# Sums of squares of the late query and key projections: one fp32 matmul replaced by two fp32r matmuls of a rounded part and its remainder

## The reference

```
def rms_norm_2(x, g):
    xf = x.astype(jnp.float32)
    y = xf * lax.rsqrt(jnp.mean(xf * xf, axis=-1, keepdims=True) + EPS) * g.astype(jnp.float32)
    return y.astype(x.dtype)

# even layer                                              # odd layer
q = rms_norm_2(dq.reshape(B, T, 16, 64), q_gain)          q = rms_norm_2(q.reshape(B, T, 32, 64), q_gain)
k = rms_norm_2(dk, k_gain)                                k = rms_norm_2(k.reshape(B, T, 4, 64), k_gain)
```

## Time and profile before

| what | value |
|---|---|
| median of 3 runs | 3009.62 us (3006.83 to 3009.97) |
| the profiled execution's own time | 3007.83 us |
| span of its instructions | 3006.0 us |
| TensorE (PE) busy | 2836.8 us, 94% of the span |
| DVE, ACT, POOL busy | 36%, 31%, 37% |
| mean granted TensorE clock | 0.969 of full |

### The profile page before, as it was taken

One profiled execution on the slowest core, in us unless ns is written; L12 is line 12 of the kernel. 1 busy time (PEld: TensorE's weight loads), 2 busy tenths in 40 slices (PEclk: granted clock), 3 DMA queues, 4 the chain that ended last, 5 costly groups with the idle time before them and its releaser, 6 DMA issues.

```text
span 3006.0 us, 34273 instructions
## 1 busy us (share of the span) xinstructions
PE 2836.8 (94%) x13922; PEld 2176.9 (72%) x13922; DVE 1091.3 (36%) x1796; ACT 927.0 (31%) x1425; POOL 1103.3 (37%) x536
## 2 busy tenths in 40 slices
PE   3679999999998997699999999999999999999999
PEld 1167688878877785357887677766788877777787
DVE  2262133113224402322221447854322465666411
ACT  2031241224124211042222322255422222666411
POOL 3043302341341330024554333444455443445443
PEclk8589999999999998799999999999999999999999
DMA  8914722231238320032434233322344333332442
GB/s 293 351 56 145 228 62 61 68 94 41 71 88 130 84 71 28 14 127 74 123 112 99 70 98 85 91 78 85 123 123 119 84 99 91 85 83 76 137 122 81
DMA packets 459337, 311.94 MB, mean 104 GB/s; under 512 B 32016, under 2 KB 412816, under 8 KB 458416
## 3 DMA queue, kind: packets, MB, share of 16 engines
q1 hardware_dynamic: 425264, 265.41, 30.8%
q10 hardware_dynamic: 33920, 44.37, 5.7%
HBM read 289.71 MB, written 32.10 MB: 107 GB/s over the span
## 4 chain that ended last, share of the span: by engine, by line
PE 89%; DMA 4%; DVE 3%; POOL 2%; ACT 1%; issue 1%; SPq 0%; ACTq 0%; DVEq 0%; POOLq 0%
PE acc L1654 75%; PE aux L1654 7%; PE ssq L1657 3%; PE ssq L1654 3%; DMA ada_ring<-in_w_ada 2%; DMA raw<-in_w_in 1%; POOL normed L1042 1%; DVE x_t L1191 1%; DVE rstd L1222 1%; PE aux L1657 1%; POOL w_lo L1053 1%; DMA masks_sb<-in_masks 1%; ACT staged L727 0%; ACT w_hi L748 0%; DVE p L1283 0%
## 5 line engine op out<-in xcount | busy, mean ns | idle before, releaser
L1053 POOL TENSOR_TENSOR w_lo<-raw,w_hi 128x1024 fp32r<-128x1024 f32 x362 | 869.7, 2403 | 1699.7 <-ACT w_hi L748 1699.7
L1654 PE MATMUL acc<-h_hi,w_hi 128*128 128x512 f32 (+1 forms) x3232 | 1211.0, 392 | 23.4 <-DVE x_t L1191 8.0
L1654 PE MATMUL acc<-h_hi,w_lo 128*128 128x512 f32 (+1 forms) x3232 | 1173.2, 380 | 0.0
L1654 PE MATMUL acc<-h_lo,w_hi 128*128 128x512 f32 (+1 forms) x2464 | 873.0, 376 | 0.8 <-issue 0.8
L748 ACT ACTIVATE w_hi<-raw 128x1024 fp32r<-128x1024 f32 x362 | 383.0, 1059 | 1166.2 <-PE acc L1654 1086.2
L1654 PEld LDWEIGHTS acc<-h_hi,w_hi 128*128 128x128 f32 x3232 | 585.7, 188 | 176.4 <-issue 52.3
L1654 PEld LDWEIGHTS acc<-h_hi,w_lo 128*128 128x128 f32 x3232 | 584.2, 188 | 118.1
L1654 PEld LDWEIGHTS acc<-h_lo,w_hi 128*128 128x128 f32 x2464 | 441.1, 189 | 94.7 <-issue 13.0
L1654 PE MATMUL acc<-out_t_lo,w_hi 128*128 128x512 f32 x768 | 298.9, 389 | 0.0
L1222 DVE RECIPROCAL rstd<-rstd 128x512 f32<-128x512 f32 (+1 forms) x29 | 118.0, 4070 | 407.0 <-ACT rstd L788 407.0
L1654 PEld LDWEIGHTS acc<-out_t_lo,w_hi 128*128 128x128 f32 x768 | 144.3, 188 | 29.1
(11 more groups left out here) (217 smaller groups left out, 2341.1 us busy)
## 6 DMA issues: line engine op xcount, KB each, us to landing
raw<-in_w_in SPq DMA_DIRECT2D x52, 1024.0 KB, 5.8
raw<-in_even_w_in SPq DMA_DIRECT2D x41, 1024.0 KB, 5.5
raw<-in_odd_w_in SPq DMA_DIRECT2D x36, 1024.0 KB, 5.6
ada_ring<-in_w_ada SPq DMA_DIRECT2D x32, 1024.0 KB, 8.7
gate_ring<-in_w_ada SPq DMA_DIRECT2D x16, 1024.0 KB, 7.1
raw<-in_w_out SPq DMA_DIRECT2D x16, 1024.0 KB, 5.9
raw<-in_even_w_out SPq DMA_DIRECT2D x16, 1024.0 KB, 5.8
raw<-in_odd_w_out SPq DMA_DIRECT2D x16, 1024.0 KB, 6.6
```

The costliest lines, as they stand in the source:

```text
L1053: G_.tensor_tensor(WL[half][:], RAW[G.rs][:, half * HALF * P:(half + 1) * HALF * P], WH[half][:].bitcast(F32), ALU.subtract).then_inc(S["l ...
L1654: return M.matmul(out_, lhsT, rhs, start=start, stop=stop, skip_group_check=True)
```

## The change

The 27 sums of squares are made by two fp32r matmuls of one pass each instead of one fp32 matmul. ACT's Square now writes the square rounded to fp32r (`squares_hi`). DVE multiplies `scaled` by itself into `squares` in full fp32 (first new instruction), waits for ACT's rounded square, and subtracts it (second new instruction), which gives the remainder (`squares_lo`) and increments a new semaphore `sq_low`. Both stand directly behind `take` on DVE, ahead of the selection rounds. TensorE waits for `sq_low` where it waited for `sq_made`, and `first` stands behind k-tile 4 instead of 3 when the previous group is of kind `norm` or `kvn`. The ones are copied once into an fp32r tile (`ones64_r`) by DVE in the group `ikw`. Some small tiles move to other addresses.

```
     SQ2, RS2 = at("squares2", SEQ, 174 * K1), at("rstd2", SEQ, 176 * K1)
+    SQH2, SQL2 = at("squares2_hi", SEQ, 194 * K1, F32R), at("squares2_lo", SEQ, 196 * K1, F32R)
+    ONESR = at("ones64_r", P, 200 * K1 + 512, F32R)
...
+        def squares(G):
+            return (SQH3, SQL3) if G.dst in ("K3", "Q3") else (SQH2, SQL2)
...
     elif G.kind in ("norm", "kvn"):                      # ACT, post
         act.wait_ge(S["taken"], G.t + 1)
         need(act, "sq_summed", G.norm)
-        A.activation(scratch(G)[0][:], Y[G.y][:], ACT.Square).then_inc(S["sq_made"], 1)
+        A.activation(squares(G)[0][:], Y[G.y][:], ACT.Square).then_inc(S["sq_made"], 1)
...
     e.then_inc(S["taken"], 1)                            # DVE, take
+    if k in ("norm", "kvn"):
+        SQ, (high, low) = scratch(G)[0], squares(G)
+        dve.wait_ge(S["taken"], G.t + 1)
+        L.link(Vv.tensor_tensor(SQ[:], Y[G.y][:], Y[G.y][:], ALU.mult))
+        dve.wait_ge(S["sq_made"], G.norm + 1)
+        need(dve, "sq_summed", G.norm)
+        Vv.tensor_tensor(low[:], SQ[:], high[:].bitcast(F32), ALU.subtract).then_inc(S["sq_low"], 1)
...
     L.done(Vv.tensor_copy(IDR[:], IDENT[:]))             # DVE, after, ikw
+    L.done(Vv.tensor_copy(ONESR[:], ONES64[:]))
...
     if k in ("norm", "kvn"):                             # TensorE, first
-        pe.wait_ge(S["sq_made"], G.norm + 1)
+        pe.wait_ge(S["sq_low"], G.norm + 1)
         need(pe, "std_made", G.norm)
-        mm(SSQ[:, 0:SEQ], ONES64[:], scratch(G)[0][:], True, True).then_inc(S["sq_summed"], 1)
+        high, low = squares(G)
+        mm(SSQ[:, 0:SEQ], ONESR[:], high[:], True, False)
+        mm(SSQ[:, 0:SEQ], ONESR[:], low[:], False, True).then_inc(S["sq_summed"], 1)
...
-    at_first = 5 if prev is not None and prev.kind == "wout" else 3
+    at_first = 3 if prev is None else {"wout": 5, "norm": 4, "kvn": 4}.get(prev.kind, 3)
```

More of the change, by code:

```diff
@@ L429, in build @@
     Y = [at(f"scaled{s}", SEQ, (201 + 2 * s) * K1) for s in range(2)]
-    LNG, LSM, LRI = (at(n, 16, 200 * K1 + 512 + 64 * i) for i, n in enumerate(("u_neg_max", "u_sum", "u_inv")))
+    LNG, LSM, LRI = (at(n, 16, 200 * K1 + 256 + 64 * i) for i, n in enumerate(("u_neg_max", "u_sum", "u_inv")))
     FIN = [at(f"final{s}", SEQ, 2 * s * K1) for s in range(2)]
@@ L445, in build @@
     PW = at("pool_w_sb", 8 * 256, 144 * K1)
-    TRI = at("tri_sb", P, 200 * K1)
+    TRI = at("tri_sb", P, 198 * K1)
     IDX, WK = at("index_score", QT * SEQ, 80 * K1), at("index_work", 3 * SEQ, 88 * K1)
@@ L455, in build @@
     SQ3, RS3 = at("squares3", SEQ, 180 * K1), at("rstd3", SEQ, 182 * K1)
+    SQH3, SQL3 = at("squares3_hi", SEQ, 184 * K1, F32R), at("squares3_lo", SEQ, 186 * K1, F32R)
     P3 = [at(f"p3_{s}", 4 * 257, 180 * K1 + 4128 * s) for s in range(3)]
     PT3 = at("p3_t", 2 * SEQ, 192 * K1 + 256)
-    T3 = [at(f"win_bias{s}", 256, 196 * K1 + 512 + s * K1) for s in range(4)]
+    T3 = [at(f"win_bias{s}", 256, 196 * K1 + 256 + s * K1) for s in range(4)]
     DST = dict(Q=Q, K=K, V=V, GATE=GATE, KD=KD, Q2=Q2, Q3=Q3)
@@ L488, in build @@
             "bias_ready", "o_hi", "o_lo", "od_hi", "od_lo",
-            "taken", "xg_hi", "xg_lo", "sq_ready", "sum_done", "rstd_ready", "gated", "sq_made", "sq_summed", "std_made",
+            "taken", "xg_hi", "xg_lo", "sq_ready", "sum_done", "rstd_ready", "gated", "sq_made", "sq_low", "sq_summed", "std_made",
             "rs_made", "normed", "y_turned", "y_copied", "pooled", "pool_mm", "py_done", "ot_hi", "ot_lo", "sel_done",
```

## The result

| | before | changed |
|---|---|---|
| median | 3008.44 us (4 runs, 3006.83 to 3009.97) | 3033.57 us (4 runs, 3030.0 to 3036.22) |
| ratio to before | | 1.0082, 95% interval 1.0067 to 1.0096 |
| span of the profiled execution | 3006.0 us | 3034.4 us |

The changed kernel is slower by 0.8%, 25 us. Forecast were 3030.7 us and a range of 3021 to 3043, with a chance of 0.90 for slower.

The account below looks back on a forecast made before the run. TensorE, 89% of the chain, was taken as the bound. 14.7 - 0.4 + 2.7 + 2.2 + 1.7 + 0.2 = +21.1 us on 3007.83 gave 3028.9, with 1.8 for the median 3030.7; range 3021 to 3043.

Parts of the forecast that it names:

- The mechanism: Sum of each group: POOL's remainder of the weights holds DVE's subtraction to about B+4.4 (B: group's first matmul); TensorE waits 1.0 us.
- The saving: TensorE's sum of squares: two single-pass matmuls cost 0.45 us instead of 0.89, saving 0.44 per group, 11.9 for 27.
- The ordinary group: Q2 tiles 1 to 5, first K3, all 16 Q3, met by an idle DVE: +0.67 us each, 22 together +14.7.
- the second key tile of the odd layer: Second K3, DVE late: product falls into POOL's operation, subtraction out at B+5.1 (B: next group's first matmul), +1.36 us.
- Q2 tile 0: First even query tile, its take without idle time before it: product and subtraction both come behind POOL's operation, +1.36 us.
- tile 6: Q2 tile behind the end of the selection: three comparisons and a held product make DVE later, +1.36 to +2.8, taken +2.2.
- the start of the attention: Q2 tile 7, attention unit 1 already waiting 2.01 us: +1.3 for the chain's delay, +0.4 for the clock, together +1.7 us.
- The clock rival: Behind each of 26 TensorE waits the lower clock costs 1.0 us: +26 on top, 3057 us; chance 0.08.
- The faster rival: DVE's subtraction is not held by POOL, out at B+2.6, TensorE waits nowhere: -11.9 us, 2998 with the copy; chance 0.06.
- DVE as the bound: Even tiles: DVE needs 12.9 us per group, more than 12.5; five tiles pay +1.36, +4 to +8, 3035 to 3039; chance 0.10.
- `kvn`: Sum of the `kvn` group: pooling matmuls before the next k-tile 0 hide the subtraction, -0.4 us (at worst +0.7).
- The copy of the ones: In group `ikw`, TensorE waits for DVE's copy of the ones: +0.2 us (0 to 0.6).

## Why the prediction was right, point by point

**The mechanism.** TensorE waits for a subtraction that POOL holds up, ordinary groups lose more than the pair saves, and it repeats without growing. Shown by the changed kernel's own rows, and by turning ACT's order round: 2.48 us became 0.69 and in the ordinary groups the wait went. That the DVE work or its load is the cost there was excluded (odd groups 11.79 us with it), and so was a pair that saves nothing (11.33 us). Only behind the selection is DVE's load itself a cost: with the same work and no wait for the remainder that tile lost 6.0 us.

**The saving.** Forecast 0.44 us for each sum, measured 0.46 (11.79 to 11.33).

**The ordinary group.** Forecast: pair at B+4.4, +0.67. Measured: B+4.46, +0.75, 22 times. POOL hardly noticed the new product: its row is 2.46 us instead of 2.38, not 2.6; it ended at B+3.86, inside the forecast window. The wait was 1.06 us instead of 1.0, and the slower start behind it cost 0.15 instead of 0.1: the pair took 0.57 us up to the next matmul instead of 0.45, and the 33 behind it 7.51 instead of 7.48. 22 x 0.08 = 1.8 us more than forecast.

**The tiles where DVE is late.** For the second key tile of the odd layer I forecast B+5.1 and +1.36; the pair starts 5.1 behind the boundary and the group costs 1.4; TensorE's bracket there is 1.57.

In the even tiles the two late terms were mis-sized. Q2 tile 0 was to cost +1.36 and cost 3.4; tile 6 was to cost +2.2 and cost 4.3. DVE's take and product of tile 0, and its last `q_t` and the take of tile 6:

```profile
1884.83 0.69 DVE L1534 TENSOR_TENSOR scaled<-acc,rstd_n 128x512 f32<-128x512 f32 x1
1885.55 2.04 DVE L1539 TENSOR_TENSOR squares<-scaled 128x512 f32<-128x512 f32 x1
```

```profile
1963.59 1.55 DVE L1603 SCALAR_TENSOR_TENSOR q_t<-scaled,cols_sb,rstd 128x512 f32<-128x512 f32 x1
1965.06 0.68 DVE L1534 TENSOR_TENSOR scaled<-acc,rstd_n 128x512 f32<-128x512 f32 x1
```

In tile 0 it is the product that comes second to POOL and takes 2.04 us; in tile 6 the take stands right behind the `q_t` that the selection had held up.

The waits that follow, on TensorE, ahead of the pair of tile 0 and of tile 1, and ahead of that of tile 6 and of attention unit 1:

```profile
1888.37 0.50 PE L1669 MATMUL ssq<-squares_hi,ones_r 128*128 128x512 f32 x1 [1.90 <-DVE squares_lo L1542]
...
1902.54 0.50 PE L1669 MATMUL ssq<-squares_hi,ones_r 128*128 128x512 f32 x1 [0.90 <-DVE squares_lo L1542]
```

```profile
1967.24 0.50 PE L1669 MATMUL ssq<-squares_hi,ones_r 128*128 128x512 f32 x1 [2.88 <-DVE squares_lo L1542]
...
1987.50 0.47 PE L1669 MATMUL acc<-select_mask,ident_r 128*128 128x256 f32 x2 [3.35 <-DVE q_t L1603]
```

And what the chain shows behind them (33 matmuls of a group, 7.53 us where the clock is full), with the windows of the clock:

```profile
1889.10 9.15 PE acc L1669 x33
...
1903.28 7.53 PE acc L1669 x33
...
1968.14 8.93 PE acc L1669 x33
```

```profile
1888.50:1891.50 3.00, 3.00 (x9) 2.38 (x10) 2.93 (x10) 0.69 (x1) 0.00 (x0) 0.61 1.10 300
1967.50:1970.50 3.00, 3.00 (x9) 2.29 (x9) 1.61 (x1) 0.69 (x1) 0.00 (x0) 0.52 1.14 326
2362.00:2365.00 3.00, 3.00 (x13) 2.49 (x14) 1.57 (x1) 0.86 (x2) 0.00 (x0) 1.00 1.11 308
2392.00:2582.00 190.00, 176.41 (x760) 141.16 (x760) 140.66 (x77) 50.86 (x61) 72.90 (x30) 1.00 0.32 86
```

Tile 0's wait of 1.90 us was followed by 33 matmuls in 9.15 us, tile 6's wait of 2.88 by 33 in 8.93: 1.6 and 1.4 us that went with the clock, at 0.61 and 0.52 of full in the first 3 us. I had given the clock to one place, the start of the attention, and counted it nowhere else short of the rival. That is the step that was off: I took the waits of the late tiles as ordinary ones, though they were about as long as, or longer than, the one wait of which the earlier trace rows had shown the price. The remaining 0.4 and 0.7 us are mostly the takes, which came later than I took them. Yet no rule by the length of the wait would have given these prices: behind 2.06 us the clock stayed at 1.00 in the kernel with ACT's order turned round and the sum behind k-tile 3, and behind 2.86 us the kernel with DVE's work alone lost 3.0 us, not 1.4. What decides whether and for how long the clock falls stays open; 3.0 of the measured microseconds hang on it.

**The clock rival.** It gave every wait a loss. In the odd tiles the clock is 1.00 over all 190 us with a wait in each group, and it is 1.00 behind the 1.57 us of the second key tile. The Trainium skill (TensorE: Matmul & The Clock Gate, "A second HAM failure mode: psum-queue depth-cycling") tells of a kernel in which frequent short idle times between groups of matmuls made the clock oscillate; 0.91 us in each 12.5 and, with the sum behind k-tile 3, 1.57 in each 13.2 did not do so here.

**The faster rival and DVE as the bound.** The first fell with the row of 2.48 us. The second: in the even tiles 1 to 5 DVE still had about 1 us idle at each boundary, and groups were 12.54 us, as forecast: the last product came behind POOL's operation in 0.75 us. At the boundaries of tile 0 and of the tile behind the selection DVE was late, as forecast.

**The rest.** `kvn` -0.4, forecast -0.4. The start of the attention +1.5, forecast +1.7; its wait was 3.35 us. The copy of the ones 0.1, forecast 0.2.

The sum by what was measured: 22 x 0.754 + 3.4 + 4.3 + 1.4 + 1.5 - 0.4 + 0.1 = 26.9, against 21.1 forecast and 25 between the medians. The two profiled executions differ by 28.4; the 1.5 left over lie ahead of the changed stretch, and cannot be put down to the change: the changed kernel and those of the experiments built from it, which have the same instructions up to there, reach the end of the `kvn` tile at times that lie up to 8.6 us apart. So that the median came within 3 us of the forecast is partly luck: in the stretch that was worked out the forecast was 5.8 us short.

## What to carry to other kernels

Replacing one matmul by two faster ones moves the question from TensorE to whoever makes the second operand: work out when that operand is ready, from the rows of every engine around the boundary, before counting the saving. An elementwise operation of DVE with two inputs in SBUF that is issued while POOL runs one costs POOL's rest plus its own tail; turning round two instructions on a third engine (here ACT's) can take it out of the way for nothing. Where a wait has a fixed end, each matmul moved ahead of it is saved in full. A wait near 2 us may cost the clock too: ask for its price, but don't count on one.

## What the runs showed of the hardware that was not expected

- A single wait of under 2 us can already be followed by the lower clock, and its length alone doesn't say whether it is. Waits with a bracket of 0.91 us (22 in the changed kernel) and 1.57 us (in nearly every group with the sum behind k-tile 3) left the clock at 1.00. Waits of 1.84, 1.90, 2.88 and 4.74 us were followed by 3 us at 0.50 to 0.61 of full. Of waits near 2 us some were followed by the lower clock (2.01 before), others not: 2.06 us with ACT's order turned round and the sum behind k-tile 3 left it at 1.00.
- The price differs as well. Behind 2.88 us of waiting in the changed kernel the clock took 1.4 us, behind 2.86 us in the kernel with DVE's work alone 3.0 us, with 6 us at 0.50.
- A sum as one fp32 matmul of 128x512 costs TensorE 0.91 us of a group, as two fp32r ones 0.45 (11.79 and 11.33 us for a group of 48 others).
- POOL's operation lost only 0.08 us of its 2.4 to a DVE product that overlapped its first 0.2 us. DVE's subtraction, issued while POOL had 1.93 us left, took 2.48 us instead of 0.69 and ended 0.55 behind POOL. In both collisions the one that was issued first kept its length.
